# Two expert-product blocks made one, and GpSimd's selections put between other subtractions

## The chip, the cores and the metric

The kernel runs on one NeuronCore of one Trainium2 chip. The metric is the time of one execution on the device, in microseconds (us). Before the change it is 2365.32 us, the median of 3 runs (2365.23 to 2368.57). The names of the engines are those of the profile: PE multiplies matrices (PEld is its load of the stationary operand), DVE is VectorE, ACT is ScalarE, POOL is GpSimd, SP is SyncE, which in this kernel only issues transfers. A "q" behind a name (SPq, ACTq) means the sequencer of that engine, which issues its DMAs.

## The reference

Two layers follow each other: one of attention and gated delta rule, and one of a recurrent mixer with a product-key mixture of experts ("peer"). The change touches the experts alone. 512 tokens of width 1024 each choose 16 experts in each of 8 heads, out of 16384; an expert is a row of `u_tab` and a row of `v_tab`:

```python
sc = einsum("thpk,hpnk->thpn", q, sub_keys)          # two lists of 128 scores per head
s_top, i_top = top_k(sc, 16)                         # 16 best of either list
cand = s_top[:, :, 0, :, None] + s_top[:, :, 1, None, :]
best, pos = top_k(cand.reshape(n_tok, 8, 256), 16)   # 16 best pairs
idx, g = expert numbers of the pairs, softmax(best)
act = gelu(einsum("phkd,pd->phk", u_tab[idx], t))    # first product
out = einsum("phk,phkd->pd", g * act, v_tab[idx])    # second product
return rmsnorm(h + out, final_g)
```

## The kernel before

**Dense and gathered experts.** Tokens 0 to 383 (`DENSE`) are computed against all experts: the tables are read in 128 tiles of 128 rows of 1024 numbers (512 KB each), and the weights of the experts that a token did not choose are zero. The last 128 tokens fetch their own 128 rows each from both tables by indirect DMAs of GpSimd (128 rows of 4 KB, 512 KB a piece, into four slots `row_slot`); VectorE multiplies and adds them. Every float32 product on PE is made of three matmuls in the faster format: the operand is split into a high half (a copy on ACT) and a low half (a subtraction on DVE or POOL), and high times high, high times low and low times high are added.

**Three stages.** Each is a block in which every engine runs its own program; at the end of a block all semaphores are cleared and the engines meet at a barrier.

1. `choose_experts` (L1324). Queries and scores are made in four steps; DVE finds the best of each step. A selection `select(i, n)` on POOL (L1570: one multiplication L1385 called at L1573, three halving additions L1575, one last L1576) turns ranks of step i into key numbers for list n. DVE prepares its input (L1677) in two arrays `eq` that all steps share: before it fills them for step i, it waits for both selections of step i-1 (L1673). The selections of step 3 are done by DVE itself (L1683, L1684). Beside that the block already computes the first product of the 16 first expert tiles (`EARLY`): tile e is transposed by PE (`turn`, L1468), copied twice by ACT (`copy`, L1512), its low half is subtracted by POOL (`low_early`, L1587), and PE multiplies (L1492); ACT applies the gelu (L1561) and SP stores the result in DRAM as `acts[e]`. ACT copies tile e only after the low half of tile e-2 is there (L1517). The exponential of the softmax (L1557) stands in ACT's program just ahead of the gelu of the last early tile; DVE's sums (L1687 and on) wait for it.
2. `first_products` (L1725): the other 112 tiles of the first product, four to a turn of the loop, over two buffers `raw` that lie in `xh`. SP loads tile j as soon as tile j-2 is transposed (L1781). During the first 96 tiles PE also spreads the weights of four tokens at a time into the dense array `u_spread` (`spread_tokens`); POOL stores a part of it in DRAM (`weights`). In each of the last 16 tiles DVE does two gathered rows instead (`twice`, L1913). ACT stores the activations (L1954), and waits for the last of these stores at the end (L1964).
3. `second_products` (L1967): 128 tiles of `v_tab`, again four buffers in `xh`. For each tile SP loads the tile (L2007), its activations `v_ga` (L2009) and its weights `v_gg` (L2010). DVE multiplies activations and weights of the next tile (`weigh_next`), then subtracts the two low halves (L2065, L2068) and adds one gathered row (L2072); ACT makes the high halves (L2115, L2117) once PE is done with the tile two before (`used`). PE adds 18 matmuls a tile into six banks (L2139). The banks are opened and closed by matmuls of zeros (L2134, L2166). Then SP loads the residual (2 MB) back into `xh`, which is free by then, and the final gain; DVE adds, ACT squares, DVE normalises (L2104) and SP stores the four output tiles.

The order of the work is written out by hand: each engine runs its list in order and waits for semaphores. A DMA of SP goes to the same queue (q1) as those ahead of it.

## Time and profile before

| | before |
|---|---|
| median of 3 runs | 2365.32 us |
| the profiled execution | 2366.43 us |
| its span | 2364.6 us |
| mean granted clock of PE, share of full speed | 0.958 |
| busy: PE, PEld, DVE, ACT, POOL | 2140.9, 1878.7, 1690.2, 818.6, 767.3 us |
| chain that ended last, PE bank L2139 | 22% |
| HBM read and written | 381.80 and 46.14 MB |

A span runs from the first to the last instruction. 1.8 us of the profiled time lie around it. The busy times are sums over the whole program; which engine is waited for differs from stage to stage, so the rows further down are taken stage by stage. "Idle before" in a row is the time in which the engine of that row stood still ahead of it, and the arrow names what ended it.

### The profile page before, as it was taken

How to read it: one execution, taken by the hardware profiler on the slowest of the kernel's cores; microseconds unless marked ns; L12 is line 12 of the kernel's file. 1: busy time of each engine (PE TensorE's matmuls, PEld its weight loads, DVE VectorE, ACT ScalarE, POOL GpSimd, SP SyncE). 2: the span in 40 equal slices, each digit the busy share in tenths (PEclk: the TensorE clock that was granted, in tenths of full speed). 3: DMA queues.
4: the chain of work that ended last, by engine and by line, in shares of the span. 5: the costliest groups of instructions: out<-in, count | busy, mean ns of one | idle time of the engine just before them, and what ended most of it. 6: DMA issues, size and time to landing. Idle time of an engine off the chain costs nothing. (4 is left out here: it accounts for less than half of the span.)

```text
span 2364.6 us, 36245 instructions
## 1 busy us (share of the span) xinstructions
PE 2140.9 (91%) x11207; PEld 1878.7 (79%) x11207; DVE 1690.2 (71%) x3352; ACT 818.6 (35%) x1408; POOL 767.3 (32%) x677
## 2 busy tenths in 40 slices
PE   5998978569999987987699999999998999999997
PEld 4776777457777766867699999999996888888885
DVE  3576544548687664699377887887876888888886
ACT  4444322222322222323334444434432333333333
POOL 1000044000000000276467887887743222222220
PEclk9999999789999998998899999999999999999999
DMA  4432100132342504302277987887698999999995
GB/s 111 88 71 36 19 1 0 51 95 74 79 113 64 137 19 135 122 18 93 69 250 226 297 275 250 293 279 245 225 320 300 335 338 336 339 336 339 337 339 198
DMA packets 229948, 428.88 MB, mean 181 GB/s; under 512 B 18516, under 2 KB 155892, under 8 KB 229620
## 3 DMA queue, kind: packets, MB, share of 16 engines
q1 hardware_dynamic: 170976, 254.85, 34.9%
q0 software_dynamic: 41472, 151.01, 18.7%
q10 hardware_dynamic: 17428, 22.14, 2.6%
q8 instruction: 34, 0.56, 0.1%
q14 instruction: 38, 0.31, 0.0%
HBM read 381.80 MB, written 46.14 MB: 181 GB/s over the span
## 5 line engine op out<-in xcount | busy, mean ns | idle before, releaser
L1859 PE MATMUL bank<-xt_hi,u_hi 128*128 128x384 f32 x896 | 309.4, 345 | 0.0
L2139 PE MATMUL bank<-xt_hi 128*128 128x512 f32 x768 | 302.3, 394 | 7.5 <-DVE xt_lo L2068 7.5
L1859 PE MATMUL bank<-xt_hi,u_lo 128*128 128x384 f32 x896 | 300.5, 335 | 0.0
L1859 PE MATMUL bank<-xt_lo,u_hi 128*128 128x384 f32 x896 | 300.2, 335 | 0.0
L2139 PE MATMUL bank<-xt_lo,xt_hi 128*128 128x512 f32 x768 | 299.9, 390 | 0.0
L2139 PE MATMUL bank<-xt_hi,xt_lo 128*128 128x512 f32 x768 | 299.7, 390 | 0.0
L1721 POOL DMA_INDIRECT row_slot<-in_peer_v_dram,row_index x128 | 138.7, 1084 | 391.9 <-DVE row_x L2072 373.8
L2115 ACT ACTIVATE xt_hi<-xh 128x1024 fp32r<-128x1024 f32 x128 | 135.9, 1061 | 338.6 <-PE bank L2139 333.0
L2065 DVE TENSOR_TENSOR xt_lo<-xh,xt_hi 128x1024 fp32r<-128x1024 f32 x128 | 156.8, 1225 | 83.7 <-ACT xt_hi L2115 83.7
L1800 POOL TENSOR_TENSOR u_two<-u_match,u_weight_hi 128x512 fp32r<-128x512 f32 x96 | 180.3, 1878 | 96.9 <-DVE u_match L1886 96.4
L1392 POOL TENSOR_TENSOR k_wlo<-k_raw,k_whi 128x2048 fp32r<-128x2048 f32 x4 | 18.4, 4602 | 588.8 <-ACT k_whi L1511 588.8
L1270 PE MATMUL bank<-xt_hi,x_whi 128*128 128x512 f32 x448 | 178.6, 399 | 12.1 <-DVE x_work L1255 9.5
L2139 PEld LDWEIGHTS bank<-xt_hi 128*128 128x128 f32 x768 | 144.8, 189 | 39.9 <-DVE xt_lo L2068 5.3
L1270 PE MATMUL bank<-xt_lo,x_whi 128*128 128x512 f32 x448 | 174.5, 389 | 0.0
L1270 PE MATMUL bank<-xt_hi,x_wlo 128*128 128x512 f32 x448 | 174.5, 389 | 0.0
L1950 ACT ACTIVATE xh<-bank 128x384 f32<-128x384 f32 x112 | 55.0, 491 | 341.5 <-PE bank L1859 338.8
L2139 PEld LDWEIGHTS bank<-xt_lo,xt_hi 128*128 128x128 f32 x768 | 144.9, 189 | 31.2 <-issue 1.2
L1859 PEld LDWEIGHTS bank<-xt_lo,u_hi 128*128 128x128 f32 x896 | 168.9, 189 | 0.0
L2139 PEld LDWEIGHTS bank<-xt_hi,xt_lo 128*128 128x128 f32 x768 | 144.8, 189 | 30.2
L1859 PEld LDWEIGHTS bank<-xt_hi,u_hi 128*128 128x128 f32 x896 | 168.8, 188 | 0.0
L1859 PEld LDWEIGHTS bank<-xt_hi,u_lo 128*128 128x128 f32 x896 | 168.4, 188 | 0.0
L1878 DVE TENSOR_TENSOR u_lo<-bank,u_hi 128x512 fp32r<-128x512 f32 x226 | 145.7, 686 | 30.4 <-ACT u_hi L1935 27.7
(420 smaller groups left out, 4880.6 us busy)
## 6 DMA issues: line engine op xcount, KB each, us to landing
xh<-in_peer_v_dram SPq DMA_DIRECT2D x128, 512.0 KB, 5.4
xh<-in_peer_u_dram SPq DMA_DIRECT2D x113, 512.0 KB
x_raw<-in_w_in_dram SPq DMA_DIRECT2D x56, 512.0 KB, 5.4
v_ga<-acts SPq DMA_DIRECT2D x128, 192.0 KB
acts<-xh ACTq DMA_DIRECT2D x112, 192.0 KB
weights<-u_spread POOLq DMA_DIRECT2D x32, 512.0 KB
v_gg<-weights SPq DMA_DIRECT2D x128, 128.0 KB
p_raw<-in_w_in_dram SPq DMA_DIRECT2D x12, 1024.0 KB
```

The costliest lines, as they stand in the source:

```text
L1270: mm = pe.matmul(k.ps[n][:, :], w[n][:, c, :], x[:, c, :], start=(c == 0 and w is whi and x is hi), stop=(c == DC - 1 and w is wlo))
L1392: eng.tensor_tensor(wlo[b][:, :, :], raw[sec % 2][:, :, :], whi[b][:, :, :].bitcast(F32), ALU.subtract).then_inc(w_lo[b], 1)
L1721: pool.indirect_dma_start(rows["slots"][n % SLOTS][:, :], None, io_rows, bass.IndirectOffsetOnAxis(ap=rows["index"][:, n:n + 1], axis=0)). ...
L1800: pool.tensor_tensor(two[b][:, :, h, :], match[:, :, :], part.unsqueeze(2).to_broadcast([P, TOK_TILE, P]), ALU.mult).then_inc(two_done, 1)
L1859: mm = pe.matmul(k.ps[4 + b][:, 0:DENSE], w[b][:, c, :], x[:, c, 0:DENSE], start=(c == 0 and w is uhi and x is hi), stop=(c == DC - 1 and ...
L1878: dve.tensor_tensor(ulo[b][:, 4 * f:4 * f + 4, :], k.ps[2 * b + f][:, :].rearrange("p (c n) -> p c n", c=4), uhi[b][:, 4 * f:4 * f + 4, :] ...
L1950: act.activation(ga[b], k.ps[4 + b][:, 0:DENSE], ACT.Gelu_apprx_tanh).then_inc(s["ga_done"][b], 1)
L2065: dve.tensor_tensor(vlo[b], raw[u], vhi[b].bitcast(F32), ALU.subtract).then_inc(slot_v[u], 1)
L2115: act.activation(vhi[b], raw[u], ACT.Copy).then_inc(s["vhi_done"][b], 1)
L2139: mm = pe.matmul(k.ps[q][:, :], h[b][:, t * P:(t + 1) * P], v[b][:, f], start=False, stop=False, skip_group_check=True)
```

## The change

- **Selections.** POOL's order in `choose_experts` alternates selections and low halves of the early tiles in another pattern. No instruction is added or removed.
- **One block.** `first_products` and `second_products` become `expert_products`. The barrier, the clearing of semaphores and ACT's wait for its last stores between them go. The second product's first four tiles are written out ahead of its loop. SP loads tile 0 of `v_tab` when the last transposes of buffer 0 are done, tile 1 likewise, and tiles 2 and 3 when the last stores of `acts` have landed, because their place in `xh` is where those stores are read from.
- **Other operands.** The split halves of the second product lie in the buffers of the first (`u_hi`, `u_lo`, `u_one`, `u_two`) instead of in `xt`.
- **Residual and gain** have buffers of their own (`v_residual`, `v_gain`) and are loaded by SP after 96 of the 112 tiles, ahead of the loop over the last 16.
- **No matmuls of zeros.** The first matmul of a bank starts it and the last one stops it, and DVE waits bank by bank (`closed`) where it waited for two banks at a time.
- DVE multiplies the gelu of the gathered dots by their weights inside the first tile, not ahead of it.

```diff
                 low(pool, 7)
-                select(1, 0)
-                select(1, 1)
...
-                for e in range(5):
+                select(1, 0)
+                for e in range(2):
+                    low_early(e)
+                select(1, 1)
+                for e in range(2, 7):
                     low_early(e)
                 select(2, 0)
-                for e in range(5, EARLY - 1):
+                for e in range(7, 9):
                     low_early(e)
                 select(2, 1)
-                low_early(EARLY - 1)
+                for e in range(9, EARLY):
+                    low_early(e)
...
+        vhi, vlo = ([x[b][:, :, :].rearrange("p c n -> p (c n)") for b in range(2)] for x in (uhi, ulo))
+        hhi = [one[b][:, :, :].rearrange("p q n -> p (q n)")[:, 0:DENSE] for b in range(2)]
+        hlo = [two[b][:, :, :, :].rearrange("p q h n -> p (q h n)")[:, 0:DENSE] for b in range(2)]
+        rest, gain = k.sb("v_residual", [P, TT, D], ctx=st), k.sb("v_gain", [P, D], ctx=st)
...
                 load(0, 0)
-                with sp.Fori(0, rounds) as n:
+                with sp.Fori(0, spread_rounds) as n:
                     for u in range(PER):
                         load(n, u + 1)
+                sp.dma_start(rest[:, :, :], residual).then_inc(res_in, 16)
+                sp.dma_start(gain[:, :], io["final_g_2"].partition_broadcast(P)).then_inc(gain_in, 16)
+                with sp.Fori(spread_rounds, rounds - 1) as n:
+                    for u in range(PER):
+                        load(n, u + 1)
+                for u in range(PER - 1):
+                    load(rounds - 1, u + 1)
...
+                for u in range(PER):
+                    if u < 2:
+                        sp.wait_ge(s["turned"][u], after(2 * uses))
+                    elif u == 2:
+                        for b in range(2):
+                            sp.wait_ge(s["ga_out"][b], after(16 * uses))
+                    load_v(0, u)
+                    load_weighting(0, u)
+                with sp.Fori(1, v_rounds) as n:
+                    for u in range(PER):
+                        sp.wait_ge(slot_v[u], after(n))
+                        load_v(n, u)
+                        sp.wait_ge(slot_h[u], after(n * 2))
+                        load_weighting(n, u)
...
+                def fetch_v(n):
+                    pool.wait_ge(dot_done, after(P))
+                    if n >= SLOTS:
+                        pool.wait_ge(summed, after(n - SLOTS + 2))
+                    fetch_row(pool, v_rows, rows, n, v_row_in)
...
+                def v_tile(n, u, start=False):
+                    b = ready(n, u)
+                    for q in range(2 * LAST):
+                        if start and q >= 4:
+                            pe.wait_ge(s["ga_done"][q - 4], after(uses))
+                        mm = weighted(b, q, start)
+                    mm.then_inc(v["used"][b], 1)
...
+                for q in range(2 * LAST):
+                    weighted(last[0], q)
+                    weighted(last[1], q, stop=True).then_inc(closed, 1)
...
                     for f in range(2):
+                        if t < LAST:
+                            dve.wait_ge(closed, 2 * t + f + 1)
...
+                        dve.tensor_tensor(rest[:, t, h], rest[:, t, h], more, ALU.add).then_inc(added, 1)
...
-                for b in range(2):
-                    act.wait_ge(s["ga_out"][b], after(16 * tiles // 2))
...
+                act.wait_ge(spread_ready, after(steps))
+                for u in range(PER):
+                    split(0, u)
+                    if u == 0:
+                        act.wait_ge(dot_done, after(P))
+                        act.activation(rows["dot"][:, :], rows["dot"][:, :], ACT.Gelu_apprx_tanh).then_inc(acted, 1)
```

The order of POOL in `choose_experts`, from the first selection of step 2 on, before (L1385, L1575 and L1576 are one selection, L1589 the low halves of early tiles):

```order
L1385 TENSOR_TENSOR xh<-xh,k_top_f 128x2048
L1575 TENSOR_TENSOR xh<-xh 128x128x8
L1575 TENSOR_TENSOR xh<-xh 128x128x4
L1575 TENSOR_TENSOR xh<-xh 128x128x2
L1576 TENSOR_TENSOR k_sel<-xh 128x128
L1589 TENSOR_TENSOR k_wlo<-k_raw,k_whi 128x1024 x10
L1385 TENSOR_TENSOR xh<-xh,k_top_f 128x2048
L1575 TENSOR_TENSOR xh<-xh 128x128x8
L1575 TENSOR_TENSOR xh<-xh 128x128x4
L1575 TENSOR_TENSOR xh<-xh 128x128x2
L1576 TENSOR_TENSOR k_sel<-xh 128x128
L1589 TENSOR_TENSOR k_wlo<-k_raw,k_whi 128x1024
```

and the same place of POOL after the change (the low halves are L1587 there):

```order
L1385 TENSOR_TENSOR xh<-xh,k_top_f 128x2048
L1575 TENSOR_TENSOR xh<-xh 128x128x8
L1575 TENSOR_TENSOR xh<-xh 128x128x4
L1575 TENSOR_TENSOR xh<-xh 128x128x2
L1576 TENSOR_TENSOR k_sel<-xh 128x128
L1587 TENSOR_TENSOR k_wlo<-k_raw,k_whi 128x1024 x2
L1385 TENSOR_TENSOR xh<-xh,k_top_f 128x2048
L1575 TENSOR_TENSOR xh<-xh 128x128x8
L1575 TENSOR_TENSOR xh<-xh 128x128x4
L1575 TENSOR_TENSOR xh<-xh 128x128x2
L1576 TENSOR_TENSOR k_sel<-xh 128x128
L1587 TENSOR_TENSOR k_wlo<-k_raw,k_whi 128x1024 x7
```

Two low halves stand between the two selections where ten stood, and seven behind them where one did. Ahead of these rows, two low halves are now between the selections of step 1 and five behind them, where five stood behind both.

SP's list where the first product ends, before:

```order
L1782 DMA xh<-in_peer_u_dram 128x1024
L1786 REGISTER_ALU
L1786 COMPARE_AND_BRANCH
L1775 UNCONDITIONAL_BRANCH
L2000 UNCONDITIONAL_BRANCH
L2002 UNCONDITIONAL_BRANCH
L2002 ISA
L2007 ISA
L2007 DMA xh<-in_peer_v_dram 128x1024
L2008 ISA
L2009 ISA
L2009 DMA v_ga<-acts 128x384
```

and after the change, from the end of the loop over the first 96 tiles (two pieces, the loop over the last tiles left out between them):

```order
L1827 COMPARE_AND_BRANCH
L1830 DMA v_residual<-residual 128x4096
L1831 DMA v_gain<-in_final_g_dram 128x1024
L1832 UNCONDITIONAL_BRANCH
L1832 ISA
L1815 ISA
L1815 DMA xh<-in_peer_u_dram 128x1024
```

```order
L1832 COMPARE_AND_BRANCH
L1815 DMA xh<-in_peer_u_dram 128x1024 x3
L1819 DMA xh<-in_peer_v_dram 128x1024
L1823 DMA v_ga<-acts 128x384
L1824 DMA v_gg<-weights 128x256
L1819 DMA xh<-in_peer_v_dram 128x1024
L1823 DMA v_ga<-acts 128x384
L1824 DMA v_gg<-weights 128x256
```

The residual and the gain stand ahead of the loads of the last `u` tiles, and the first `v` tiles directly behind the last `u` tile with no barrier between.

## Rows read from the trace of the kernel before

**Rows 1.** Timeline of POOL in choose_experts: start, us, engine, line, op, count [idle before].
```profile
1046.48 6.51 POOL L1385 TENSOR_TENSOR xh<-xh,k_top_f 128x2048 f32<-128x2048 f32 x1 [13.77 <-DVE xh L1677]
...
1067.24 7.10 POOL L1589 TENSOR_TENSOR k_wlo<-k_raw,k_whi 128x1024 fp32r<-128x1024 f32 x3
...
1089.91 6.59 POOL L1385 TENSOR_TENSOR xh<-xh,k_top_f 128x2048 f32<-128x2048 f32 x1 [3.41 <-DVE xh L1677]
...
1101.37 7.00 POOL L1589 TENSOR_TENSOR k_wlo<-k_raw,k_whi 128x1024 fp32r<-128x1024 f32 x3
...
1147.24 4.60 POOL L1385 TENSOR_TENSOR xh<-xh,k_top_f 128x2048 f32<-128x2048 f32 x1
...
1156.77 2.34 POOL L1589 TENSOR_TENSOR k_wlo<-k_raw,k_whi 128x1024 fp32r<-128x1024 f32 x1
```

**Rows 2.** Timeline of DVE in choose_experts, around the last step.
```profile
1122.52 0.29 DVE L1670 TENSOR_TENSOR k_rank<-k_rank,k_eighth 128x128 f32<-128x128 f32 x1
1156.92 6.54 DVE L1677 TENSOR_TENSOR xh<-k_rank,row 128x2048 f32<-128x2048 f32 x2 [34.11 <-POOL k_sel L1576]
...
1172.42 0.68 DVE L1687 TENSOR_REDUCE k_total<-k_best 128x32 f32<-128x512 f32 x1
...
1174.59 1.30 DVE L1701 COPY xh<-k_sel 128x128 f32<-128x128 f32 x9
```

**Rows 3.** Timeline of ACT in choose_experts: gelu of early tiles 5 and 12, exponential, last copy.
```profile
1110.04 0.49 ACT L1561 ACTIVATE k_t<-bank 128x384 f32<-128x384 f32 x1 [4.18 <-PE bank L1492]
...
1146.92 0.49 ACT L1561 ACTIVATE k_t<-bank 128x384 f32<-128x384 f32 x1 [2.11 <-PE bank L1492]
...
1156.66 1.28 ACT L1557 ACT_TABLE_LOAD   x1
1157.95 0.63 ACT L1557 ACTIVATE k_best<-k_best 128x512 f32<-128x512 f32 x1
...
1178.16 0.49 ACT L1564 ACTIVATE chosen<-bank 128x384 f32<-128x384 f32 x1
```

**Rows 4.** Timeline of PE: start of early tile 5's product.
```profile
1103.77 0.69 PE L1492 MATMUL bank<-xt_hi,k_whi 128*128 128x384 f32 x1 [5.94 <-POOL k_wlo L1589]
```

**Rows 5.** Timeline of PE: end of the first product, start of the second, last two tiles.
```profile
1798.54 0.34 PE L1859 MATMUL bank<-xt_hi,u_lo 128*128 128x384 f32 x1
...
1817.75 0.79 PE L2139 MATMUL bank<-xt_hi 128*128 128x512 f32 x1 [4.51 <-DVE xt_lo L2068]
...
2336.71 0.77 PE L2139 MATMUL bank<-xt_hi 128*128 128x512 f32 x1 [3.02 <-DVE xt_lo L2068]
```

**Rows 6.** Timeline of ACT's sequencer: the last store of activations.
```profile
1799.58 0.34 ACTq L1954 DMA_DIRECT2D acts<-xh  x1
```

**Rows 7.** Timeline of DVE: last dot, first work of the second product, and the end.
```profile
1798.04 1.22 DVE L1898 SCALAR_TENSOR_TENSOR row_slot<-row_slot,row_x 128x1024 f32<-128x1024 f32 x1
...
1804.94 0.91 DVE L2039 MEMSET row_x<- 128x1024 f32 x1 [0.16 <-issue]
...
1815.46 0.42 DVE L2056 TENSOR_TENSOR v_h<-v_ga,v_gg 128x256 f32<-128x256 f32 x1 [4.95 <-DMA v_gg<-weights]
...
2344.42 1.29 DVE L2091 TENSOR_TENSOR xh<-xh,row_x 128x512 f32<-128x512 f32 x2 [6.66 <-DMA xh<-residual]
...
2359.23 1.28 DVE L2104 SCALAR_TENSOR_TENSOR u_spread<-xh,v_stat,u_spread 128x1024 f32<-128x1024 f32 x1
```

**Rows 8.** Chain that ended last, in order of time: start, us, what (two transfers).
```profile
1807.11 8.15 DMA v_gg<-weights
...
2336.25 8.15 DMA xh<-residual
```

**Rows 9.** Windows: stretch, busy us (instructions) of PE, PEld, DVE, ACT, POOL; clock, DMA share, GB/s.
```profile
1716.00:1799.40 83.40, 82.88 (x525) 82.09 (x523) 60.77 (x101) 26.44 (x51) 35.08 (x29) 1.00 0.89 316
1818.00:2334.00 516.00, 515.68 (x2268) 426.51 (x2268) 432.62 (x631) 184.38 (x251) 133.87 (x124) 1.00 0.95 332
```

**Rows 10.** Waits from 1700 to 1799 us: waiter, waited for; us, times, longest.
```profile
DVE row_slot L1898 <- DMA row_slot<-in_peer_u_dram,row_index: 3.8, 8, 1.0
```

More of the change, by code:

```diff
@@ new lines, in split @@
+                def split(n, u):
+                    b, before = place(n, u)
+                    act.wait_ge(v_in[u], after(n * 16 + 16))
+                    if isinstance(n, int) and u < 2:
+                        act.wait_ge(s["product"][b], after(uses))
+                    act.wait_ge(v["used"][b], after(before))
+                    act.activation(vhi[b], v_raw[u], ACT.Copy).then_inc(v["vhi_done"][b], 1)
+                    act.wait_ge(slot_h[u], after(n * 2 + 2))
+                    act.activation(hhi[b], h32[b][:, :], ACT.Copy).then_inc(v["hhi_done"][b], 1)
```

312 lines of the change are left out of this document (136 added, 176 removed).

## The prediction

> **What bounds the kernel now.** I first read the windows by stage, then the timeline of every engine at the places where PE stands still, then the chain of waits for the end. PE is the limit in both products: in the last 16 tiles of the first it is busy 82.88 of 83.40 us, in the second 515.68 of 516.00 us, both at full clock [rows 9]. Nothing is to be gained inside them. What can be gained lies around them, in three places. In `choose_experts` DVE stands still for 34.1 us until POOL has done the second selection of step 2 [rows 2]. Between the products PE is idle from 1798.9 (1798.54 + 0.34) to 1817.75 but for its matmuls of zeros, so 18.9 us without useful work [rows 5]. At the end DVE waits 6.66 us for the residual, which is asked for only at 2336.25 and takes 8.15 us [rows 7, 8].
>
> **Selections.** Durations: a selection takes 9.5 us (1147.24 to 1156.77), the one that runs beside DVE's L1677 11.4 (1089.91 to 1101.37), three low halves 7.0 to 7.1, so 2.37 each [rows 1]. A product of one early tile takes 6.3 us when PE comes from a long wait (1103.77 to the gelu at 1110.04) [rows 3, 4]; in a stretch without a wait gelus follow every 5.27 us (1110.04 to 1146.92 is 7 tiles) [rows 3].
> Step by step on POOL: the first selection of step 1 starts at 1046.5 as now and ends at 1057.8 (9.4 before the 1067.24 of rows 1). The low halves of tiles 0 and 1 follow, at 1060.2 and 1062.6; now the first is there at 1069.6. The second selection runs to 1072.1, low half 2 is ready at 1074.5. PE: tile 0 from 1060.2 to 1066.5, tile 1 to 1071.7, waits to 1074.5, tile 2 to 1080.2, tile 6 to about 1101. The first selection of step 2 begins when DVE has filled its input, at 1089.9 as now, because that is DVE's own pace, and ends at 1101.4. Low half 7 is ready at 1103.8: PE starts tile 7 where it now starts tile 5. Low half 8 at 1106.1, then the second selection to 1115.6, where it now ends at 1156.8. Low half 9 at 1118.0; tile 9 to 1123.9, and six tiles at 5.27 give tile 15 at 1155.5.
> DVE has its ranks at 1122.8 [rows 2] and no longer waits. Its next work, 1156.92 to 1172.42, is 15.5 us and ends at 1138.3. Then it needs the exponential, which ACT's program keeps ahead of the last gelu: tile 14's gelu ends at 1150.7, a table load and the exponential (0.63) bring it to 1152.7 with 1.28 for the load [rows 3]. DVE's sums and copies, 1172.42 to 1175.89, are 3.5 us: 1156.2. From there to the last copy of ACT it is 2.76 us now (1175.89 to 1178.65) [rows 2, 3]: 1158.9, where it is 1178.65 now. **Gain 20 us.** So the 34 us are not all gained: early tiles become the limit behind them. Bounds: if PE never waits for a low half it is 22; if the last six tiles take half a us longer each and the waits for low halves 7 and 9 half a us too, 16.
>
> **From first to second product.** Everything that PE's first matmul needs, counted from the last dot of DVE, which ends at 1799.3 [rows 7]: clearing `row_x` 0.9, the multiplication for tile 0 in two parts (0.42 and a shorter one, 0.7), then the stretch that now goes from 1815.46 to PE's start at 1817.75, 2.3 us: next tile's multiplication and two low halves [rows 5, 7]. Sum 1803.2. ACT's copy is not later: its last store is issued at 1799.6 to 1799.9 [rows 6], the high half of tile 0 is ready at 1801. The transfers: tile 0 of `v_tab` is asked for at the last transposes of its buffer, 10 us before the end; tile 1 with its weights 5 us before, at about 1795.6 for the last piece. The transfer of the same piece took 8.15 us in the cold start with four gathers beside it [rows 8]; taken so, it lands at 1803.8 and PE starts at 1806.0; with 5 us it is hidden. I take 1804.0, nearer the lower end, since the gathers have been asked for by then and run out. So 13.7 us gained. Zeros cost nothing now (they end before 1817.75), so their removal here gives nothing.
> Then a wait that is new: the weights of tile 2 are asked for only when ACT's last store has landed, and DVE needs them ahead of the low half of tile 1. Store landed at about 1802 (my estimate; it lies between 1799.9 and the barrier's 1804), pieces issued by 1803.1, landed 5 to 8.15 us later [rows 8], 2.3 us of DVE: 1810.4 to 1813.5. PE has done tile 0 6 us after its start, at 1810: 18 matmuls at 0.2275 us are 4.1, and the lower clock after a wait costs 2 more (the 6.3 us of early tile 5 against 5.27 less 0.9 for its transposes). Cost 0.4 to 3.5; I take 2. **Gain 12 us**, bounds 8 and 15.
>
> **The residual's new place.** 2.1 MB and 0.5 MB go into q1 ahead of the tile loads, in the stretch that already moves 316 GB/s [rows 9] and in which DVE waits for gathered rows 8 times, 3.8 us in all [rows 10]. A tile asked for just behind it must be there two tiles later: 525 matmuls are 16.4 tiles of 32, so 5.05 us a tile and 10.1 for two. Gathers need 1.05 MB and stores 0.2 MB in 5.05 us, 247 GB/s. If the residual gets only what they leave of 332 GB/s it takes 31 us and delays several tiles; if it displaces them it takes 8.15 [rows 8] plus 1.6, and the tile is in time. In the first case gathers are in time and tiles late, in the second the other way round, and DVE has 1.4 us a tile to spare. At no slack the price is all of 2.62 MB at 316 GB/s, 8.3 us; at full slack 0. I take 3: the stretch is near its limit but 22.6 us of DVE and 11% of DMA time are free in it. **Loss 3 us**, bounds 0 and 8.
> The Trainium skill (DMA: Bandwidth & Descriptors, section Specifications) gives about 358 GB/s as what HBM yields to a core. By it the 27.3 MB of these 16 tiles and 2.6 more need 83.5 us where PE needs 81, a loss of 2.5 us by an estimate from that page. No row here shows more than 332 over a long stretch.
>
> **The end.** DVE's chain from the first addition to the last output, 2344.42 to 2360.51, is 16.1 us [rows 7]. It can start 6.66 earlier, at 2337.8. PE starts the last two tiles at 2336.71 [rows 5]; 36 matmuls at 0.2275 us (515.68 us for 2268) and the same 2 us for the lower clock at first end at 2346.9, one bank every 1.4 us. The second bank closes at 2341.7, and DVE, which would want it at 2339, waits; after that each output takes DVE 3.6 us and the banks are ahead. Last output at 2354.5. **Gain 6 us**, bounds 5 and 6.7. With the zeros kept the third pair would close at about 2352, which DVE would wait for; that is what their removal saves here.
>
> **Sum.** -20 -12 +3 -6 = -35. From the profiled execution's 2366.4: 2331.4. The median of the runs shown is 1.1 lower, so 2330.3.
>
> **Rivals.**
> (a) The residual is paid in full, 8.3 us for 3, because u tiles queue behind it and gathers lag too. For it: waits for rows exist already. Against: PE has no wait in that stretch. 2336. The skill (same page, Queues, rings and completion order) says that an engine of the DMA consumes a ring in order, which makes this case possible; no row here shows two transfers of q1 overtaking or not.
> (b) POOL's two selections of step 2 come as close to PE as the low halves: the waits at tiles 7 and 9 grow by 3 us each, because ACT's copies hang on the low half two tiles before. Gain 14: 2336.
> (c) The second product starts as cold as before: transfers, not the barrier, were its limit (4.95 us of DVE's wait in rows 7 are for `v_gg`). Gain 4 to 6 for 12: 2337.
> (d) Slower. The second product moves 332 GB/s with the DMA engines 95% busy [rows 9], 4.09 us a tile. If after the change a tile took 0.27 us longer, because operands in other buffers or loads that never get ahead keep PE waiting, 128 of them would cost the 35 us; from there on it is slower. Against it: SP waits for free buffers now, so transfers are ahead, and no transfer or matmul of the loop is changed in size. 2370 or more.
> (e) PE's and DVE's gains don't reach the end, time unchanged: only if stages overlapped, which a barrier after `choose_experts` excludes.
>
> **Chances.** Forecast 0.64; (a) 0.12; (b) 0.10; (c) 0.10; (d) 0.02; (e) 0.02. With my own range 2324 to 2336 for the forecast and the others at 2336 to 2342, 2321 to 2343 holds 8 in 10 and somewhat more. A measurement of this kernel tells about 0.2% (5 us) from no change: faster 0.96, within 0.2% 0.02, slower 0.02.
>
> **What would show it.** Selections: DVE's idle ahead of L1677 of the last step gone, PE's two waits for low halves at about 1101 to 1104 and 1115 to 1118, last copy into `chosen` near 1159. Products: PE idle 5 us between the last u matmul and the first v matmul, perhaps 2 before tile 1. Residual: waits of PE for u tiles or of DVE for `row_slot` in the last 16 tiles. End: no wait of DVE for the residual, one of 1 to 3 us for a bank, last output 18 us after the last two tiles start. I am wrong if the DMA rate of the second product falls under 332 GB/s, or if the stage after the selections starts later than 1165.

## The result, and the profile after

| | before | after |
|---|---|---|
| median of the runs, us | 2366.06 (2365.23 to 2368.57, 4 runs) | 2329.61 (2323.23 to 2331.24, 4 runs) |
| span of the profiled run, us | 2364.6 | 2327.2 |
| time of the profiled run, us | 2366.43 | 2328.99 |

The changed kernel takes 0.9839 of the time before, 95% interval 0.9819 to 0.9859. Forecast were 2330.3 us and -35; measured are -36.5 between the medians and -37.4 between the two profiled executions.

To see where they come from I cut both traces at the same seven places: the start of POOL's first selection of step 1 (S0), the end of ACT's last copy into `chosen` (S1), the first `u_hi` of the next stage on ACT (S2), the end of the last u matmul (S3), the first v matmul (S4), PE's start on the last two tiles (S5), the end of DVE's last output (S6).

| us | up to S0 | S0-S1 | S1-S2 | S2-S3 | S3-S4 | S4-S5 | S5-S6 | S0-S6 |
|---|---|---|---|---|---|---|---|---|
| before | 1046.5 | 132.2 | 7.0 | 613.2 | 18.9 | 519.0 | 23.8 | 1314.0 |
| after | 1044.7 | 110.4 | 8.1 | 613.5 | 5.6 | 523.4 | 17.5 | 1278.5 |
| difference | -1.8 | -21.8 | +1.1 | +0.3 | -13.3 | +4.4 | -6.3 | -35.5 |

The code up to S0 is the same in both. That place moved between 1043.9 and 1052.7 us over the thirteen profiled runs of this document, so the columns to the right of it say more than a single time does.

**Selections.** The waits from 1040 to 1156 us of the changed kernel (waiter, waited for: us in total, times, longest):
```profile
DVE k_total L1690 <- ACT k_best L1557: 10.9, 1, 10.9
PE bank L1492 <- POOL k_wlo L1587: 10.0, 4, 2.7
```
DVE's 34.11 us ahead of its last comparisons [rows 2] are gone. In its timeline the comparisons follow at once, and a later wait has taken part of the place, for the exponential:
```profile
1122.90 6.69 DVE L1680 TENSOR_TENSOR xh<-k_rank,row 128x2048 f32<-128x2048 f32 x2
...
1149.50 0.69 DVE L1690 TENSOR_REDUCE k_total<-k_best 128x32 f32<-128x512 f32 x1 [10.88 <-ACT k_best L1557]
```
ACT's timeline: the exponential stands ahead of the last gelu, and the last copies end at 1155.06, where they ended at 1178.65 [rows 3]:
```profile
1147.54 1.28 ACT L1557 ACT_TABLE_LOAD   x1
1148.83 0.63 ACT L1557 ACTIVATE k_best<-k_best 128x512 f32<-128x512 f32 x1
...
1151.19 0.49 ACT L1561 ACTIVATE k_t<-bank 128x384 f32<-128x384 f32 x1 [0.42 <-PE bank L1492]
1153.62 1.44 ACT L1564 ACTIVATE chosen<-bank 128x384 f32<-128x384 f32 x3 [1.94 <-PE bank L1499]
```
PE's waits for low halves were three before, 20.3 us in all, with the 5.94 us of [rows 4] among them (window 1040 to 1180 us):
```profile
PE bank L1492 <- POOL k_wlo L1589: 20.3, 3, 11.3
```
They have become four of 2 to 2.7 us, at the places that the working gave; the fourth, of 2.60 us, is at 1115.95:
```profile
1058.45 0.69 PE L1492 MATMUL bank<-xt_hi,k_whi 128*128 128x384 f32 x1 [1.98 <-POOL k_wlo L1587]
...
1073.02 0.44 PE L1492 MATMUL bank<-xt_hi,k_whi 128*128 128x384 f32 x1 [2.74 <-POOL k_wlo L1587]
...
1101.40 0.44 PE L1492 MATMUL bank<-xt_hi,k_whi 128*128 128x384 f32 x1 [2.72 <-POOL k_wlo L1587]
```

**Between the products.** PE's timeline, to be read beside [rows 5]. The distance of starts shows the clock: a matmul starts every 0.43 us from 1782.86, every 0.23 us from 1785.36, and every 0.43 us again from 1792.33 to 1795.32.
```profile
1782.30 0.77 PE L1957 MATMUL bank<-u_hi,u_one 128*128 128x512 f32 x1 [5.59 <-DVE u_two L2074]
...
1790.76 0.47 PE L1957 MATMUL bank<-u_hi,u_one 128*128 128x512 f32 x1 [2.73 <-DVE u_two L2074]
```
The windows of the two slow stretches (columns as in [rows 9]; the clock is the last but two) show a granted clock of half, 1.2 GHz, in both:
```profile
1782.30:1785.40 3.10, 3.10 (x8) 2.49 (x9) 0.00 (x0) 0.00 (x0) 2.07 (x3) 0.52 1.01 361
1792.30:1795.60 3.30, 3.30 (x9) 2.58 (x8) 3.30 (x6) 0.00 (x0) 2.18 (x1) 0.51 1.04 399
```
DVE's timeline, beside [rows 7]. The weights are there when the last dot is done (1777.11 + 1.23), and nothing is waited for until the first gathered row of the second table:
```profile
1777.11 1.23 DVE L2016 SCALAR_TENSOR_TENSOR row_slot<-row_slot,row_x 128x1024 f32<-128x1024 f32 x1 [0.57 <-DMA row_slot<-in_peer_u_dram,row_index]
...
1781.60 0.55 DVE L2074 TENSOR_TENSOR u_two<-v_h,u_one 128x384 fp32r<-128x384 f32 x1
1786.86 0.29 DVE L2079 TENSOR_TENSOR row_dot<-row_dot,row_weight 128x128 f32<-128x128 f32 x1 [4.71 <-DMA row_slot<-in_peer_v_dram,row_index]
```

**The two products.** Windows (stretch; busy us and instructions of PE, PEld, DVE, ACT, POOL; clock, DMA share, GB/s): the last u tiles and the second product, beside [rows 9].
```profile
1694.00:1775.00 81.00, 80.64 (x510) 79.98 (x509) 57.29 (x95) 24.88 (x48) 36.67 (x29) 1.00 0.94 344
1800.00:2296.00 496.00, 496.00 (x2190) 410.85 (x2189) 416.20 (x609) 179.79 (x244) 114.14 (x121) 1.00 0.96 337
```

**The end.** DVE waits for nothing ahead of the residual's addition, where it waited 6.66 us [rows 7], and the last output starts 16.2 us after PE's start on the last two tiles, where it was 22.5.
```profile
2306.83 1.30 DVE L2104 TENSOR_TENSOR v_residual<-v_residual,row_x 128x512 f32<-128x512 f32 x2
2308.04 1.36 DVE L2104 TENSOR_TENSOR v_residual<-v_residual,bank 128x512 f32<-128x512 f32 x2
2311.03 0.15 DVE L116 TENSOR_SCALAR v_stat<-v_stat 128x1 f32<-128x1 f32 x1 [1.63 <-ACT v_stat L2184]
...
2321.92 1.28 DVE L2117 SCALAR_TENSOR_TENSOR u_spread<-v_residual,v_stat,v_gain 128x1024 f32<-128x1024 f32 x1
```

### The profile page after: what moved, and what is told of

It is laid out like the page before. It is cut to its first block, busy times and chain, and to the rows that moved or that the text cites. A ratio compares the mean times of both kernels' runs of the same rounds, so it can differ in the third digit from the quotient of the medians.

```text
span 2327.2 us, 36155 instructions
## 1 busy us (share of the span) xinstructions
PE 2125.3 (91%) x11175; PEld 1872.0 (80%) x11175; DVE 1690.2 (73%) x3349; ACT 817.7 (35%) x1406; POOL 756.6 (33%) x677
## 4 chain that ended last, share of the span: by engine, by line
PE 47%; DMA 2%; DVE 1%; issue 0%; ACT 0%; POOL 0%; ACTq 0%; DVEq 0%; SPq 0%
PE bank L1957 22%; PE bank L1940 19%; PE bank L1921 4%; PE bank L1929 2%; DMA xh<-in_peer_u_dram 1%; DMA row_slot<-in_peer_u_dram,row_index 1%; DMA row_slot<-in_peer_v_dram,row_index 0%; DVE u_spread L2117 0%; DVE v_residual L2104 0%; DVE row_slot L2016 0%; POOL row_slot L1724 0%; ACT L2184 0%; DVE row_x L2082 0%; DVE u_lo L2071 0%; ACT u_spread L2182 0%
## 5 line engine op out<-in xcount | busy, mean ns | idle before, releaser
L1957 PE MATMUL bank<-u_hi,u_one 128*128 128x512 f32 x768 | 300.4, 391 | 11.3 <-DVE u_two L2074 11.3
L1957 PE MATMUL bank<-u_hi,u_two 128*128 128x512 f32 x768 | 299.9, 390 | 0.0
L1957 PE MATMUL bank<-u_lo,u_one 128*128 128x512 f32 x768 | 299.8, 390 | 0.0
L2163 ACT ACTIVATE u_hi<-xh 128x1024 fp32r<-128x1024 f32 x128 | 135.8, 1061 | 336.9 <-PE bank L1957 329.1
L1724 POOL DMA_INDIRECT row_slot<-in_peer_v_dram,row_index x128 | 124.4, 972 | 398.0 <-DVE row_x L2082 371.0
L2071 DVE TENSOR_TENSOR u_lo<-xh,u_hi 128x1024 fp32r<-128x1024 f32 x128 | 156.8, 1225 | 83.9 <-ACT u_hi L2163 83.9
L1957 PEld LDWEIGHTS bank<-u_hi,u_one 128*128 128x128 f32 x768 | 144.9, 189 | 42.5 <-issue 9.3
L1957 PEld LDWEIGHTS bank<-u_lo,u_one 128*128 128x128 f32 x768 | 145.0, 189 | 30.1
L1957 PEld LDWEIGHTS bank<-u_hi,u_two 128*128 128x128 f32 x768 | 144.9, 189 | 30.1
```

The source lines that it names most:

```text
L1724: pool.indirect_dma_start(rows["slots"][n % SLOTS][:, :], None, io_rows, bass.IndirectOffsetOnAxis(ap=rows["index"][:, n:n + 1], axis=0)). ...
L1957: mm = pe.matmul(k.ps[q][:, :], h[b][:, t * P:(t + 1) * P], w[b][:, f], start=start and h is hhi and w is vhi, stop=stop and h is hlo, ski ...
L2071: dve.tensor_tensor(vlo[b], v_raw[u], vhi[b].bitcast(F32), ALU.subtract).then_inc(slot_v[u], 1)
L2163: act.activation(vhi[b], v_raw[u], ACT.Copy).then_inc(v["vhi_done"][b], 1)
```

## The experiments

Ratios are to the kernel before, measured on the same chip at the same time. The segments of every profiled run, cut at the same places:

| us | S0 at | S0-S1 | S1-S2 | S2-S3 | S3-S4 | S4-S5 | S5-S6 | S0-S6 |
|---|---|---|---|---|---|---|---|---|
| after_again | 1043.9 | 110.5 | 8.0 | 613.5 | 5.8 | 522.1 | 17.5 | 1277.4 |
| only_selections | 1046.1 | 110.4 | 7.0 | 613.0 | 19.6 | 519.5 | 23.4 | 1292.9 |
| only_one_block | 1049.7 | 132.3 | 8.0 | 613.8 | 6.1 | 522.9 | 17.5 | 1300.6 |
| row_later | 1049.1 | 110.3 | 8.1 | 615.0 | 5.2 | 520.4 | 17.5 | 1276.4 |
| residual_late | 1046.8 | 110.3 | 8.2 | 613.0 | 6.8 | 521.7 | 24.5 | 1284.5 |
| more_traffic | 1044.6 | 110.0 | 8.2 | 628.8 | 6.6 | 521.8 | 17.5 | 1292.9 |
| zeros_at_close | 1045.3 | 110.1 | 8.2 | 613.0 | 5.9 | 521.4 | 20.7 | 1279.4 |
| split_selections | 1045.4 | 107.5 | 8.2 | 615.3 | 5.2 | 520.8 | 18.3 | 1275.3 |
| early_exp | 1049.0 | 108.2 | 9.2 | 613.0 | 6.5 | 522.0 | 17.5 | 1276.5 |
| short_pool_ops | 1045.9 | 108.3 | 8.1 | 613.3 | 6.4 | 522.0 | 17.5 | 1275.5 |
| short_and_row_later | 1052.7 | 108.5 | 8.3 | 613.1 | 5.5 | 520.6 | 17.5 | 1273.5 |

**The changed kernel once more (after_again).** No edit; it gives the spread.

> The changed kernel once more, as the measure for the others. The parts read from the two traces (changes of the distance between fixed points of the program) add up to -37: selections -20.6, from the last u matmul to the first v matmul -13.3, the residual's new place +0.3, a new wait at tile 1 of the second product with the lower clock behind it +4.4, the end -6.3. Expected 0.984 of before, 2323 to 2332 us.

Measured: 2328.9 us, ratio 0.9838 (0.9825 to 0.9852). Between two traces of the same kernel the segments agree within 0.2 us, but for S4-S5 (1.3).

**The order on POOL alone (only_selections).** The kernel before with this one edit:
```diff
-                select(1, 0)
-                select(1, 1)
...
+                select(1, 0)
+                for e in range(2):
+                    low_early(e)
+                select(1, 1)
+                for e in range(2, 7):
+                    low_early(e)
...
```

> The kernel before with the new order of GpSimd's list alone, two blocks kept. Theory A (the parts are independent and add): the gain read in that stage, 20.6 us, arrives at the end whole, about 2345. Theory B (part of the early start is given back later, since the next stage waits for its first transfers): 17 to 19, about 2348. DVE has no wait ahead of its last step in either; it waits for the exponential instead (about 11 us).

Measured: 2344.9 us, ratio 0.9907 (0.9893 to 0.9920), so 0.93 points of the 1.62. S0-S1 is 110.4, the other segments are within 0.8 us of those of before. The 21.8 us belong to this order, and they arrive at the end whole, as theory A has it.

**One block alone (only_one_block).** The changed kernel with POOL's old order.
```diff
+                select(1, 0)
+                select(1, 1)
...
-                select(1, 0)
-                for e in range(2):
-                    low_early(e)
-                select(1, 1)
...
```

> The changed kernel with GpSimd's old order: one block, early residual, no zeros. Theory A: -37 + 20.6 = -16.4, about 2350. Theory B: 13 to 14, about 2352. The step from the last u matmul to the first v matmul stays at 5.6 us, the wait ahead of tile 1 at 2.7.

Measured: 2354.34 us, ratio 0.9942 (0.9928 to 0.9955), 0.58 points. The two parts together are 1.51 points against 1.62: within the intervals they add up. The step from the last u matmul to the first v matmul is 6.1 us, and PE's wait ahead of tile 1 is 3.08 us. S1-S2 is 8.0 here and 7.0 in only_selections, so the 1 us that the next stage starts later comes with the one block, not with the selections. Which of its parts does it, no run here tells.

**The first gathered row later (row_later).** DVE's first addition of a gathered row goes behind the low halves of tile 1.
```diff
+                        if isinstance(n, int) and n == 0 and u == 0:
+                            return
+                        if isinstance(n, int) and n == 0 and u == 1:
+                            v_row(0, 0)
+                        v_row(n, u)
...
```

> The changed kernel with DVE's addition of the first gathered v row (and the product of dots and weights) put behind the low halves of tile 1. Theory G (what the trace names): DVE stood 4.7 us at the first gathered row and thereby made tile 1 late; then PE's wait of 2.7 us ahead of tile 1 goes, and with it the lower clock inside tile 1: 3 to 4.5 us faster than the changed kernel. Theory W (my prediction's): the weights of tile 2 land too late for the low halves of tile 1; then DVE waits for v_gg in the same place, PE's wait stays at 2 us or more, and the time with it (within 1 us).

Measured: 2328.63 us, ratio 0.9832 (0.9818 to 0.9845). PE's wait ahead of tile 1 is gone, and S4-S5 is 520.4 for 523.4 and 522.1. So in these traces the gathered row made the wait. Behind it stood the wait that the prediction had named, in DVE's timeline:
```profile
1790.97 0.42 DVE L2062 TENSOR_TENSOR v_h<-v_ga,v_gg 128x256 f32<-128x256 f32 x1 [3.51 <-DMA v_gg<-weights]
```
PE doesn't wait for it in this run. S2-S3 is 1.5 us longer here, where the edit has no part. The wait's going is in the trace; how much of the 2 to 3 us comes with it is less sure, since split_selections, without this edit, has 520.8. The times can't tell the gain from nothing.

**The residual at the end (residual_late).** The two transfers leave the first product and go behind the last tile loads of the second.
```diff
-                sp.dma_start(rest[:, :, :], residual).then_inc(res_in, 16)
...
+                for u in range(PER):
+                    sp.wait_ge(slot_v[u], after(v_rounds))
+                    sp.wait_ge(slot_h[u], after(2 * v_rounds))
+                sp.dma_start(rest[:, :, :], residual).then_inc(res_in, 16)
...
```

> The changed kernel with the loads of the residual and the gain put back behind the last v tile, after the same waits as before the change. Theory A (from the traces): the transfer of 8 us comes back ahead of the last chain on DVE, +6.0 to +6.6 us, and the last 16 u tiles win at most 0.5 us; in total +6 against the changed kernel. Theory P (my prediction's price): the early place costs 3 us in the tail, so the net is +3. The trace decides by the time from the start of the last two tiles to the last output, and by the length of the first product.

Measured: 2337.72 us, ratio 0.9872 (0.9857 to 0.9888). That is 0.34 points above after_again, some 8 us, where theory A said 6; S0-S6 is 6.0 to 7.1 us longer than in the two traces of the changed kernel. DVE waits 7.04 us at the end, S5-S6 is 6.9 longer, and S2-S3 only 0.5 shorter. More than that half a microsecond the residual doesn't cost in its new place. It may cost nothing: zeros_at_close and early_exp have the early residual and the same 613.0 us in S2-S3.
```profile
2314.91 1.29 DVE L2107 TENSOR_TENSOR v_residual<-v_residual,row_x 128x512 f32<-128x512 f32 x2 [7.04 <-DMA v_residual<-residual]
```

**More in the same place (more_traffic).** Two further copies of 2.1 MB, from DRAM to DRAM, directly behind the residual and the gain.
```diff
+                for i in range(2):
+                    sp.dma_start(extra[i], residual).then_inc(spare_in, 16)
...
```

> The changed kernel with two more transfers behind the residual and the gain in SP's queue: each copies the residual (2.1 MB) from DRAM to DRAM; the copies are used by nobody. Theory S (slack): the residual cost only 0.3 us because gathers and u tiles have two tiles of time ahead; a backlog of 16 us more is past that slack, PE waits for u tiles or DVE for rows, and the first product becomes 5 to 14 us longer. Theory F (free capacity): the DMA engines have room for it beside the tail, the first product grows by under 2 us.

Measured: 2344.32 us, ratio 0.9907 (0.9892 to 0.9923). S2-S3 is 15.3 us longer, a little more than the 5 to 14 of theory S. PE's waits from 1160 to 1800 us, first of the changed kernel, then of this one; the 7.5 us of the changed kernel are the start of the stage.
```profile
PE bank L1921 <- DMA xh<-in_peer_u_dram: 8.1, 3, 7.5
```
```profile
PE bank L1926 <- DMA xh<-in_peer_u_dram: 21.5, 2, 13.9
```
It is one wait of 13.9 us, for the first u tile that stands behind the copies in SP's queue, and PE has no wait for tiles afterwards. So what is late is the tile behind the long transfers, and the residual alone is short enough for the two tiles that PE has ahead of it. Whether the place in the queue or the 4.2 MB themselves make it late isn't separated: no run sends the copies by another queue.

**Zeros where a bank closes (zeros_at_close).** The matmul of zeros that closed each bank before is put back; DVE clears its buffer of zeros once (0.48 us), ahead of tile 0.
```diff
-                    weighted(last[1], q, stop=True).then_inc(closed, 1)
+                    weighted(last[1], q)
+                    pe.matmul(k.ps[q][:, :], zero[:, 0:P], zero[:, :], start=False, stop=True, skip_group_check=True).then_inc(closed, 1)
```

> The changed kernel with every bank closed by a matmul of zeros again (0.87 us a bank in the kernel before, 5.2 for six). Prediction's theory: the last pair closes 5 us later, DVE waits for it, +2 to +3 us. Rival: DVE's own chain is late enough, +0 to +0.5. Reckoned from the changed kernel's trace: the last bank would close at about 2319.4, and DVE wants it at 2317.8, so +1.6.

Measured: 2329.23 us, ratio 0.9839 (0.9826 to 0.9853), the same as without. In the trace S5-S6 is 3.2 us longer, near the +2 to +3 of the prediction's theory and above the reckoned 1.6. DVE waits for banks in four places, the longest:
```profile
2310.34 0.69 DVE L2108 TENSOR_TENSOR v_residual<-v_residual,bank 128x512 f32<-128x512 f32 x1 [1.84 <-PE bank L1991]
```
The removal of the zeros is worth at most these 3 us of the 6.3, with the residual early; the times don't confirm it.

This trace shows one thing more, at the start of the second product, where the program differs by the one clearing of 0.48 us. The first gathered row is in time (DVE waits 0.15 us for it), and DVE waits ahead of tile 1's low halves for the weights of tile 2, and again for the next ones:
```profile
1786.73 0.42 DVE L2066 TENSOR_TENSOR v_h<-v_ga,v_gg 128x256 f32<-128x256 f32 x1 [2.59 <-DMA v_gg<-weights]
```
PE stands 0.58 and 1.17 us behind it. That is the wait that the prediction had named.

**Selections in halves (split_selections).** Each of POOL's last three selections is cut into its multiplication and its additions, with low halves between, and the exponential is taken two tiles earlier.
```diff
-                    if e == EARLY - 1:
+                    if e == EARLY - 3:
...
+                select(1, 0)
+                lows_early(0, 2)
+                pick_keys(1, 1)
+                lows_early(2, 3)
+                halve(1, 1)
+                lows_early(3, 8)
+                pick_keys(2, 0)
...
```

> The changed kernel with each of the last three selections on GpSimd cut in two (the multiplication, then the halving additions), low halves of early tiles between, and the exponential two tiles earlier in ACT's list. Theory L (what is left in this stage is PE's waits for low halves and ACT's copies behind them): the waits ahead of early tiles 2, 7 and 9, 2.7 us each with the lower clock behind them, mostly go, and the stage ends 7 to 11 us earlier. Rival D (DVE's own chain is next): the stage can't end before DVE's last step, and GpSimd's later end of the second selection of step 2 makes DVE wait; the gain is 0 to 3 us.

Measured: 2326.01 us, ratio 0.982 (0.9807 to 0.9834). S0-S1 is 107.5, only 2.9 shorter, where theory L said 7 to 11 and rival D 0 to 3. The last early gelu ends at 1140.48, 11 us earlier than in the changed kernel, and PE no longer limits the stage. DVE has fallen back, though not by the wait for a selection that rival D named: its last comparisons start at 1133.14, not at 1122.90. DVE's timeline in split_selections, then POOL's:
```profile
1109.38 9.77 DVE L1654 TENSOR_TENSOR k_cand<-k_top 128x128 f32<-128x128 f32 x3
...
1129.77 2.48 DVE L1682 SCALAR_TENSOR_TENSOR k_eighth<-k_eighth 128x128 f32<-128x128 f32 x1
...
1133.14 4.49 DVE L1692 TENSOR_TENSOR xh<-k_rank,row 128x2048 f32<-128x2048 f32 x2
```
```profile
1109.21 2.49 POOL L1593 TENSOR_TENSOR k_wlo<-k_raw,k_whi 128x1024 fp32r<-128x1024 f32 x1 [0.44 <-ACT k_whi L1525]
1111.65 4.66 POOL L1385 TENSOR_TENSOR xh<-xh,k_top_f 128x2048 f32<-128x2048 f32 x1
1116.39 2.67 POOL L1593 TENSOR_TENSOR k_wlo<-k_raw,k_whi 128x1024 fp32r<-128x1024 f32 x1
...
1129.64 2.46 POOL L1593 TENSOR_TENSOR k_wlo<-k_raw,k_whi 128x1024 fp32r<-128x1024 f32 x1 [1.01 <-ACT k_whi L1525]
```
Three additions of DVE last 9.77 us and end at 1119.15, when three instructions of POOL end (1119.06). A small instruction of DVE lasts 2.48 us and ends at 1132.25, when POOL's ends (1132.10); the same form takes 0.28 us in the changed kernel, with POOL idle. The program has no dependence between them there. This gave a new theory: a DVE instruction with two inputs waits until the instruction that POOL is in has ended, and gets in one at a time. Of the next two runs the first tests the exponential by itself, the second this theory.

**The exponential alone (early_exp).** The changed kernel with one line:
```diff
-                    if e == EARLY - 1:
+                    if e == EARLY - 3:
```

> The changed kernel with one edit: ACT takes the exponential of choose_experts ahead of the gelu of early tile 13 instead of that of tile 15. In the changed kernel DVE idles 10.88 us for it, at 1149.50. Theory C (the chain to chosen goes through DVE and through PE's early products at once, and the later one decides): DVE's 10.88 us shrink to under 5, but the last early gelu stays at about 1151.2 and PE's last transposes stand behind the last early product, so chosen comes only 1 to 2 us earlier; time 2327.5 to 2330 us, ratio to the kernel before 0.983 to 0.984. Rival E (DVE's wait for the exponential is the whole of it): chosen comes 5 us or more earlier, time 2322 to 2325 us, ratio 0.981 to 0.982.

Measured: 2327.35 us, ratio 0.982 (0.9803 to 0.9837). DVE's wait falls to 4.08 us, S0-S1 by 2.2 us, not by 6.8. The last gelu now ends just ahead of the last copies, in ACT's timeline:
```profile
1155.61 0.49 ACT L1561 ACTIVATE k_t<-bank 128x384 f32<-128x384 f32 x1 [3.67 <-PE bank L1492]
1155.99 1.25 ACT L1564 ACTIVATE chosen<-bank 128x384 f32<-128x384 f32 x3
```
So PE's early products end the stage here, as theory C has it. The ratio is that of rival E, a little lower than C said (0.983 to 0.984), and its interval holds both; the segments decide for C.

**Shorter instructions on POOL (short_pool_ops).** split_selections with:
```diff
-                    order(pick(pool, i, n))
+                    for q in range(0, pairs, pairs // 4):
+                        q = slice(q, q + pairs // 4)
+                        order.add(pool.tensor_tensor(eq[n][:, q, :, :], eq[n][:, q, :, :],
...
+                    for q in (slice(0, T), slice(T, 2 * T)):
+                        ins = pool.tensor_tensor(u_lo[e % 4][:, q], u_turn[e % 2][:, q], u_hi[e % 4].bitcast(F32)[:, q], ALU.subtract)
+                    ins.then_inc(u_low, 1)
```

> split_selections with POOL's long instructions cut: each multiplication of 128x2048 in four of 128x512, each early low half of 128x1024 in two of 128x512. Nothing else moves. Time 2318 to 2323 us, ratio 0.978 to 0.981. Rival G (the slowing goes with the bytes that POOL moves meanwhile, or it is a wait for a buffer): the three additions still take 8 to 10 us, and the time is 2326 to 2328 us, ratio 0.982 to 0.983.

Measured: 2327.02 us, ratio 0.9816 (0.9799 to 0.9832). DVE's timeline, then one row of POOL's, a low half in two pieces, 1.27 us each:
```profile
1110.47 4.24 DVE L1660 TENSOR_TENSOR k_cand<-k_top 128x128 f32<-128x128 f32 x3
...
1127.46 1.26 DVE L1689 TENSOR_TENSOR k_rank<-k_rank,k_eighth 128x128 f32<-128x128 f32 x1
1128.65 1.37 DVE L1690 TENSOR_TENSOR k_eighth<-k_eighth 128x128 f32<-128x128 f32 x1
1130.05 1.26 DVE L1691 TENSOR_TENSOR k_rank<-k_rank,k_eighth 128x128 f32<-128x128 f32 x1
1131.34 6.56 DVE L1698 TENSOR_TENSOR xh<-k_rank,row 128x2048 f32<-128x2048 f32 x2
```
```profile
1127.24 11.80 POOL L1598 TENSOR_TENSOR k_wlo<-k_raw,k_whi 128x512 fp32r<-128x512 f32 x6
```
```profile
1119.68 2.54 POOL L1598 TENSOR_TENSOR k_wlo<-k_raw,k_whi 128x512 fp32r<-128x512 f32 x2
```
The mechanism holds: the three additions fall from 9.77 to 4.24 us, above the 3.5 that theory F allowed, and against the 8 to 10 of rival G. Three instructions with two inputs that took 0.28 to 0.29 us each in split_selections now take 1.26 to 1.37, one piece of POOL. The sum of theory F fails, and the time is the one that rival G gave (2326 to 2328 us): POOL is busy nearly without a gap, so more of DVE's instructions meet it, and the comparisons start at 1131.34, 1.8 us earlier instead of 7 to 10. S0-S1 is 108.3, no shorter than in split_selections.

**Both (short_and_row_later).** The edits of short_pool_ops and of row_later.

> short_pool_ops, and DVE's first gathered-row addition of the second product moved behind tile 1's low halves as in row_later. The stretch from the second product's first matmul to the start of its last two tiles should be 1 to 3 us shorter than in short_pool_ops, as row_later's was (520.35 against 523.4 and 522.1 us); if the two gains are independent, time 2316 to 2322 us and ratio 0.977 to 0.980. If row_later's gain was nothing but noise, the time is that of short_pool_ops.

Measured: 2327.91 us, ratio 0.9816 (0.9797 to 0.9834). The forecast of 2316 to 2322 us failed; the time is that of short_pool_ops. S4-S5 is 1.4 us shorter than there, as row_later's was, and PE has no wait ahead of tile 1. S0-S6 is the shortest of all, 1273.5 against 1278.5 and 1277.4 in the changed kernel. But the intervals of the ratios of the last four kernels overlap with that of the changed kernel: none of them is shown to be faster.

## Why the prediction was right

The sum was -35 and the traces give -37.4, of which -1.8 lie ahead of anything that was changed. The mechanisms were right in the main, but two terms were off by some 3 us, in opposite directions. By its steps:

**Selections: -21.8 for -20.** The steps were right one by one: PE's waits at 1058.45, 1073.02 and 1101.40, and the end of the second selection of step 2 at 1113.56, answer to 1060.2, 1074.5, 1103.8 and 1115.6 of the working with 1.8 us less at the start. The gelu of early tile 9 starts at 1121.99 for 1122.1, counted in that way. DVE's ranks were ready at 1122.90, which is 1.9 us later than so counted, and cost nothing, since early tiles and the exponential became the limit behind DVE's wait, as worked out. What was too high is the way from tile 9 to the end: five tiles took 25.0 us and not 26.4, which is 1.3 us, and from the end of DVE's copies to ACT's last copy it was 2.1 us and not 2.76. early_exp shows that the stage has two ends within 3 us of one another, DVE's and PE's, and split_selections that relief for PE is taken back by DVE.

**From first to second product: -13.3 for -13.7, then +4.4 for +2.** The first matmul came 5.6 us after the last of the first product. The tile's transfers were hidden. From the end of the last dot it took 3.96 us, for the 3.9 of the working; but the last dot ended 1.6 us after the last u matmul, where it had been 0.4, and the 0.8 us that the prediction had added for a transfer covered most of that.

The loss after it had another cause in this trace than the one named. The prediction put it on the weights of tile 2; here the first gathered row was late. POOL's timeline shows when it is asked for:
```profile
1778.62 2.00 POOL L1724 DMA_INDIRECT row_slot<-in_peer_v_dram,row_index  x1 [8.95 <-DVE row_slot L2016]
```
It lands 8.22 us later by the chain of waits. DVE's program has the addition of that row ahead of the low halves of tile 1, and row_later, which moves it, takes PE's wait away. zeros_at_close has the other case: the row is there 4.2 us after its issue, and the weights of tile 2 hold PE up, as predicted. So both waits lie close together, and the prediction knew one of them.

The gather is asked for so late by the program's own order: `fetch_v` waits for all 128 dots (`dot_done`), though the slot of the first row is free three dots earlier, in DVE's timeline:
```profile
1770.74 1.23 DVE L2016 SCALAR_TENSOR_TENSOR row_slot<-row_slot,row_x 128x1024 f32<-128x1024 f32 x1 [0.32 <-DMA row_slot<-in_peer_u_dram,row_index]
```
Asked for at 1771.97, it would land at about 1780.2 by the same 8.22 us (an estimate), ahead of 1782.15, when DVE comes to it. No run tests this.

Of the 4.4 us, 2.73 are PE's wait. The rest is the second stretch at half clock, about 8 matmuls every 0.43 instead of 0.23 us, 1.6 us. In after_again the wait is 1.53 us, the clock is at half in one piece of 6.2 us from the first v matmul on, and S4-S5 is 522.1. The prediction had a clock's price only for the starts ahead of the first tile and of the last two.

**The residual's new place: +0.3 for +3.** This is the term that was mis-sized most. I took the 316 GB/s of [rows 9] for close to a limit of the whole stretch. They are a mean over two unlike parts. Windows of before, around the place where SP now asks for the residual (22 us earlier in the changed kernel), and then the same place of after:
```profile
1702.00:1716.00 14.00, 14.00 (x92) 14.00 (x90) 11.78 (x22) 5.85 (x13) 10.07 (x9) 1.00 0.68 223
1716.00:1728.00 12.00, 12.00 (x79) 11.93 (x78) 9.05 (x16) 3.84 (x8) 3.98 (x4) 1.00 0.71 244
1728.00:1791.00 63.00, 63.00 (x402) 62.63 (x401) 44.58 (x75) 20.54 (x39) 30.16 (x25) 1.00 0.97 346
```
```profile
1680.00:1694.00 14.00, 14.00 (x92) 14.00 (x91) 11.62 (x22) 6.02 (x14) 10.23 (x9) 1.00 0.90 340
```
The residual is asked for at 1681.13 and landed 10.2 us later, in the part that before moved 223 GB/s and after moves 340. The busy part at 346 GB/s comes behind it. What the residual would cost there, no run shows. The same 97 us at the end of the first product as one window, of before, then of after:
```profile
1702.00:1798.90 96.90, 96.88 (x615) 96.09 (x612) 72.19 (x121) 31.81 (x63) 45.16 (x38) 1.00 0.86 304
```
```profile
1680.00:1776.70 96.70, 96.34 (x608) 95.37 (x606) 70.15 (x118) 30.91 (x62) 46.90 (x38) 1.00 0.94 343
```
3.7 MB more went through in the same time, and S2-S3 is 0.3 us longer. The Trainium skill (DMA: Bandwidth & Descriptors, section Specifications) gives about 358 GB/s for a core: by it, as an estimate, the 33.2 MB of this stretch take 92.7 us, less than PE's 96.7, and nothing is lost. The trace agrees in that. It doesn't show 358 GB/s as a ceiling: from 1784 to 1799 us after moves 396 GB/s. The 2.5 us that I had worked out from that page came from 27.3 MB in 81 us; [rows 9] give 26.4 MB in 83.4 us, and with 2.6 MB more these take 81 us by the same figure, so no loss. more_traffic bounds the claim: 4.2 MB more at once cost 15.3 us, nearly all of it in one wait for one tile.

**The end: -6.3 for -6.** In the profiled execution DVE never waited for a bank, though 1 to 3 us were expected: PE's last two tiles kept the full clock after their 3.03 us of idle time. That holds for this one execution. In after_again the clock is at half there, and DVE waits 0.49 and 0.77 us for banks; in seven more runs with this end it waits 1.4 to 2.4 us for them. S5-S6 is 17.5 us all the same (18.3 in split_selections): where DVE doesn't wait for a bank, it waits 1.63 us for ACT's `v_stat`. So the expected wait came in eight of nine executions, and cost nothing.

**Not foreseen: +1.1** at the start of the stage after the selections, tied to the one block, its cause open.

**The rivals.** (a) is refuted by residual_late (0.5 us at most), (b) by S0-S1 and by PE's waits of 2.72 and 2.60 us at tiles 7 and 9, (c) by the 5.6 us, (d) by the window of the second product, 337 GB/s with PE busy in all of 496 us, (e) by the time. The misses of the terms between S0 and S6 are -1.8, +3.1 (+2.8 before rounding), -2.7, -0.3 and +1.1. They largely cancel, and that is luck: the total was closer than its parts.

## What to carry to other kernels

Before a transfer is put into a busy stretch, cut that stretch into short windows and look at the rate and DMA share at the very place: a mean of 316 GB/s at a share of 0.89 looked like a limit, but at its start and just ahead of it lay 26 us at 223 to 244 GB/s, into which 2.6 MB went for at most 0.5 us. When a wait of 34 us is taken away, work out which two chains come next and how far apart they are; here they lay within 3 us, so every further gain on one was taken by the other. When work starts earlier behind a merged boundary, look at what in the next stage's programs stands behind a transfer, and at what each request for a transfer waits for: here all gathers of the second table wait for the last dot, though the first needs a slot that is free three dots earlier.

## What the runs showed of the hardware

- **DVE beside POOL.** A small DVE instruction with two inputs that meets a running POOL instruction ends when that one ends: 2.48 us for 0.28 beside one of 2.46, 1.26 for 0.29 beside pieces of 1.27. A COPY with one input was held up too, 1.60 us in split_selections and 1.93 in short_pool_ops for 0.18. DVE's searches (0.23 to 0.24 us) stayed as they were. The profile counts the waiting as busy time of DVE and names no releaser; only the ends of the two engines' instructions, side by side, show it. The Trainium skill (SBUF — State Buffer, section SBUF: two separate sides) says that the two share a pair of ports as an exclusive lock, which the one that starts first holds for its whole instruction; the traces agree, with long POOL instructions and with short ones. Cutting POOL's instructions shortens each wait and multiplies their number, and gained nothing here.
- **The clock after a short wait isn't fixed by the wait.** Ahead of the first v matmul PE waits 4.5 to 6.8 us, and in all thirteen traces it comes back at half its clock, for 3 to 6.2 us. Ahead of the last two tiles it waits 3.02 to 3.14 us, and after that the clock was at half for 2.9 to 6 us in twelve traces, at once or up to 1.2 us later, and full in one, that of the changed kernel. After the waits ahead of tile 1, 0.6 to 3.1 us, it stayed full in eight traces and fell in one, again that of the changed kernel, 1.2 us after PE had resumed. The last tiles of the changed kernel, then of after_again, which is the same program:
```profile
2305.70:2308.70 3.00, 3.00 (x13) 2.49 (x14) 2.90 (x4) 0.46 (x1) 0.00 (x0) 1.00 0.02 5
```
```profile
2303.80:2306.80 3.00, 3.00 (x8) 2.38 (x9) 2.41 (x4) 0.50 (x1) 0.00 (x0) 0.52 0.02 5
```
- **A tile behind a long transfer.** Behind 6.8 MB in one queue (4.2 of them from DRAM to DRAM) a tile made PE wait 13.9 us; behind 2.6 MB it didn't.
- **A spread from upstream.** With the same program up to there, the selections began between 1043.9 and 1052.7 us, and between the two runs at the ends of that range 5.3 us of these 8.8 are there already at POOL's first long wait:
```profile
POOL a_dist L522 <- POOLq L102: 171.4, 1, 171.4
```
```profile
POOL a_dist L522 <- POOLq L102: 176.7, 1, 176.7
```
The first is after_again, the second short_and_row_later. The spread is larger than any gain of the last four kernels.
